# Attention weights times values in a two-layer encoder: padded 128-column values against two 64-column tiles side by side

## What is computed

```python
scores = einsum("bnqkgd,bnskd->bnkgqs", q, kb) * scale        # blocks of 128 queries, up to 3 blocks of keys
scores = where(valid, scores + bias, -inf)                    # window of 128, a slope per head
m = maximum(max(scores, -1), sink_b)
p = exp(scores - m)
denom = sum(p, -1) + exp(sink_b - m)
o = einsum("bnkgqs,bnskd->bnqkgd", p / denom, vb)
```

## Time and profile before

| | us |
|---|---|
| median of 3 runs | 1838.14 (1838.01 to 1838.23) |
| profiled execution, its time | 1838.19 |
| profiled execution, span | 1836.4 |
| granted TensorE clock, mean over the span | 0.997 of 2.4 GHz |
| attention loop, layer 0 | 458.8 to 508.5 of the span |
| attention loop, layer 1 | 1361.8 to 1411.5 of the span |

### The profile page before, as it was taken

One profiled execution on the slowest core, in us unless ns is written; L12 is line 12 of the kernel. 1 busy time (PEld: TensorE's weight loads), 2 busy tenths in 40 slices (PEclk: granted clock), 3 DMA queues, 4 the chain that ended last, 5 costly groups with the idle time before them and its releaser, 6 DMA issues.

```text
span 1836.4 us, 24082 instructions
## 1 busy us (share of the span) xinstructions
PE 1800.0 (98%) x8080; PEld 1477.4 (80%) x8080; DVE 895.9 (49%) x1169; ACT 749.4 (41%) x990; POOL 1062.6 (58%) x533
## 2 busy tenths in 40 slices
PE   7999999999899999999999999999998999999997
PEld 5888888888588888888888888888876888888886
DVE  6545432268776444432254444322797654444223
ACT  6333332246865333332243333223576643333221
POOL 5444457769656444457744444676784854444673
PEclk9999999999999999999999999999999999999998
DMA  4332323321113323223332322333211233222331
GB/s 172 104 102 91 99 71 100 110 98 64 46 47 104 103 91 103 82 79 98 121 104 91 98 96 81 87 101 124 69 47 47 81 103 100 94 92 82 87 100 64
DMA packets 53427, 166.73 MB, mean 91 GB/s; under 512 B 6000, under 2 KB 6256, under 8 KB 53360
## 3 DMA queue, kind: packets, MB, share of 16 engines
q1 hardware_dynamic: 52128, 163.78, 28.3%
q10 hardware_dynamic: 1232, 2.10, 0.3%
HBM read 163.76 MB, written 2.10 MB: 90 GB/s over the span
## 4 chain that ended last, share of the span: by engine, by line
issue 42%; POOL 32%; PE 23%; POOLq 2%; DVE 1%; ACT 1%; DMA 0%; ACTq 0%; DVEq 0%
POOL w_lo L413 26%; PE bank L1211 7%; PE bank L1212 7%; PE bank L1213 7%; POOL y_conv L464 3%; POOL sq_sum L422 2%; POOLq L412 1%; PE bank L1373 1%; POOL x L533 1%; POOL r_wide L489 0%; DVE glu L1146 0%; POOLq L426 0%; DVE result L1201 0%; PE bank L1383 0%; PE bank L1247 0%
## 5 line engine op out<-in xcount | busy, mean ns | idle before, releaser
L413 POOL TENSOR_TENSOR w_lo<-stage,w_hi 128x1024 fp32r<-128x1024 f32 x352 | 871.3, 2476 | 701.8 <-ACT w_hi L548 701.7
L548 ACT ACTIVATE w_hi<-stage 128x1024 fp32r<-128x1024 f32 x352 | 372.4, 1060 | 894.0 <-PE bank L1213 892.5
L1211 PE MATMUL bank<-xs_hi,w_hi 128*128 128x512 f32 (+1 forms) x1704 | 663.5, 389 | 0.0
L1213 PE MATMUL bank<-xs_hi,w_lo 128*128 128x512 f32 (+1 forms) x1704 | 659.7, 387 | 0.0
L1212 PE MATMUL bank<-xs_lo,w_hi 128*128 128x512 f32 (+1 forms) x1704 | 659.6, 387 | 0.0
L1211 PEld LDWEIGHTS bank<-xs_hi,w_hi 128*128 128x128 f32 x1704 | 320.0, 188 | 66.7 <-issue 1.9
L1212 PEld LDWEIGHTS bank<-xs_lo,w_hi 128*128 128x128 f32 x1704 | 320.0, 188 | 66.1 <-issue 1.9
L1213 PEld LDWEIGHTS bank<-xs_hi,w_lo 128*128 128x128 f32 x1704 | 319.9, 188 | 65.8
L845 DVE TENSOR_TENSOR work<-bank,rstd 128x512 f32<-128x512 f32 x176 | 120.9, 690 | 403.6 <-PE bank L1213 402.7
L1211 PE MATMUL bank<-h_hi,w_hi 128*128 128x512 f32 x704 | 273.9, 389 | 0.0
L1212 PE MATMUL bank<-h_lo,w_hi 128*128 128x512 f32 x704 | 273.9, 389 | 0.0
(11 more groups left out here) (151 smaller groups left out, 1221.7 us busy)
## 6 DMA issues: line engine op xcount, KB each, us to landing
stage<-w_gu SPq DMA_DIRECT2D x176, 512.0 KB, 3.3
stage<-w_down SPq DMA_DIRECT2D x64, 384.0 KB, 3.2
stage<-w_down SPq DMA_DIRECT2D x64, 320.0 KB, 2.9
stage<-w_in SPq DMA_DIRECT2D x24, 512.0 KB, 3.3
stage<-w_out SPq DMA_DIRECT2D x16, 512.0 KB, 3.3
x<-xT ACTq DMA_DIRECT2D x4, 512.0 KB, 7.0
stage<-w_in SPq DMA_DIRECT2D x8, 256.0 KB, 2.7
out<-result SPq DMA_DIRECT2D x8, 256.0 KB, 2.2
```

The lines of the kernel that those rows point to most:

```text
L413: nc.gpsimd.tensor_tensor(w_lo[:, r, :], stage[:, r, :], w_hi[:, r, :].bitcast(F32), ALU.subtract).then_inc(split, 1)
L548: nc.scalar.activation(w_hi[:, r, :], stage[:, r, :], ACT.Copy).then_inc(hi_made, 1)
L1211: nc.tensor.matmul(to, wh, mh, start=first, stop=False)
L1213: return nc.tensor.matmul(to, wl, mh, start=False, stop=last)
```

## The change

The values lose their padding. `v` has 128 columns per key block, 64 of each key/value head, copied in one ACT instruction. `weigh_values` now takes a block `b` and does both heads: for each key block a product with 64 columns of weights for kv 0 into partitions 0 to 63 of `side_bank`, and one for kv 1 into partitions 64 to 127, each at its column position of the array. It is called at `c == 2` of groups 2, 4 and 6 (units 10, 18, 26) and once behind the loop, in place of seven calls at `c == 3` and one behind the loop. `pt` has 3 slots instead of 2, and the waits for a free slot count blocks. `o_made` rises once a block. `widen` and `r_wide` go: `spread_denominators` reads each reciprocal as a 64-column broadcast, again in two halves, 8 products instead of 4, and waits for DVE's reciprocals instead of POOL.

```diff
+PT_SLOTS = 3
-WIDEN_IN = [1, 3, 5, 6]
...
-            pt = sb("pt", [P, 2, 3, GROUP, P], F32, region)
+            pt = sb("pt", [P, PT_SLOTS, 3, GROUP, P], F32, region)
...
-            v = sb("v", [P, NB, N_KV_HEADS, P], F32, region)
+            v = sb("v", [P, NB, P], F32, region)
...
-            r_wide = sb("r_wide", [P, GROUP, N_KV_HEADS, HEAD_DIM], F32, region)
...
-                def widen(b):
-
-                    pool.wait_ge(r_den_made, l * NB + b + 1)
-                    if b:
-                        pool.wait_ge(factors_spread, l * NB + b)
-                    for kv in range(N_KV_HEADS):
-                        nc.gpsimd.tensor_tensor(r_wide[:, :, kv, :],
...
-                    if g in WIDEN_IN:
-                        widen(WIDEN_IN.index(g))
...
-                    if g >= 2 and c == 0:
-                        act.wait_ge(o_made, l * N_GROUPS + g - 1)
+                    if g >= PT_SLOTS and c == 0:
+                        act.wait_ge(o_made, l * NB + (g - PT_SLOTS) // 2 + 1)
...
-                    nc.scalar.activation(pt[:, g % 2, 0:n, c, :], src, ACT.Copy).then_inc(pt_made, 1)
+                    nc.scalar.activation(pt[:, g % PT_SLOTS, 0:n, c, :], src, ACT.Copy).then_inc(pt_made, 1)
...
-                for kv in range(N_KV_HEADS):
-                    at = slice(HEAD_DIM * kv, HEAD_DIM * (kv + 1))
-                    nc.scalar.activation(v[:, :, kv, at], side_bank[:].rearrange("p (b d) -> p b d", d=P)[:, :, at],
-                                         ACT.Copy).then_inc(v_made, 1)
+                nc.scalar.activation(v[:], side_bank[:].rearrange("p (b d) -> p b d", d=P), ACT.Copy).then_inc(v_made, 1)
...
-                    dve.wait_ge(o_made, l * N_GROUPS + 2 * b + 2)
+                    dve.wait_ge(o_made, l * NB + b + 1)
...
-                    nc.vector.memset(v[:, :, kv, other], 0.0).then_inc(v_made, 1)
...
-                def weigh_values(g):
+                def weigh_values(b):
...
-                    pe.wait_ge(pt_made, l * N_UNITS + (g + 1) * GROUP)
-                    if b and not kv:
+                    pe.wait_ge(pt_made, l * N_UNITS + (b + 1) * 2 * GROUP)
+                    if b:
                         pe.wait_ge(o_evicted, l * NB + b)
                     for i in range(n):
-                        last = nc.tensor.matmul(side_bank[:], v[:, first + i, kv, :],
-                                                pt[:, g % 2, i, :, :].rearrange("p c q -> p (c q)"),
-                                                start=not kv and i == 0, stop=bool(kv) and i == n - 1)
+                        for kv in range(N_KV_HEADS):
+                            rows = slice(HEAD_DIM * kv, HEAD_DIM * (kv + 1))
+                            last = nc.tensor.matmul(side_bank[rows, :], v[:, first + i, rows],
+                                                    pt[:, (2 * b + kv) % PT_SLOTS, i, :, :].rearrange("p c q -> p (c q)"),
+                                                    start=i == 0, stop=i == n - 1, tile_position=(0, HEAD_DIM * kv))
                     last.then_inc(o_made, 1)
...
-                    pe.wait_ge(r_widened, (l * NB + b + 1) * N_KV_HEADS)
+                    pe.wait_ge(r_den_made, l * NB + b + 1)
                     bank_taken(ATT["spread", b, 0])
                     for c in range(GROUP):
-                        last = nc.tensor.matmul(att_bank("spread", b, 0)[:, c * P:(c + 1) * P],
-                                                r_wide[:, c, :, :].rearrange("p h d -> p (h d)"),
-                                                ident[:], start=True, stop=True)
+                        for kv in range(N_KV_HEADS):
+                            rows = slice(HEAD_DIM * kv, HEAD_DIM * (kv + 1))
+                            last = nc.tensor.matmul(att_bank("spread", b, 0)[rows, c * P:(c + 1) * P],
+                                                    r_den[:, 2 * b + kv, c:c + 1].to_broadcast([P, HEAD_DIM]),
+                                                    ident[:], start=True, stop=True, tile_position=(0, HEAD_DIM * kv))
                     last.then_inc(factors_spread, 1)
...
-                        pe.wait_ge(v_made, l * 4 + 4)
-                    if c == 3 and g:
-                        weigh_values(g - 1)
+                        pe.wait_ge(v_made, l + 1)
+                    if c == 2 and g and g % 2 == 0:
+                        weigh_values(g // 2 - 1)
...
-                weigh_values(N_GROUPS - 1)
+                weigh_values(NB - 1)
```

More of the change, by code:

```diff
@@ L283, in encoder @@
         factors_spread = sem("factors_spread")
-        r_widened = sem("r_widened")
         factors_kept = sem("factors_kept")
@@ L481, in denominators @@
                                             ALU.add).then_inc(den_made, 1)
-                def widen(b):
-                    pool.wait_ge(r_den_made, l * NB + b + 1)
-                    if b:
-                        pool.wait_ge(factors_spread, l * NB + b)
-                    for kv in range(N_KV_HEADS):
-                        nc.gpsimd.tensor_tensor(r_wide[:, :, kv, :],
-                                                r_den[:, 2 * b + kv, :].unsqueeze(2).to_broadcast([P, GROUP, HEAD_DIM]),
-                                                zero[:, 0:1].unsqueeze(2).to_broadcast([P, GROUP, HEAD_DIM]),
-                                                ALU.add).then_inc(r_widened, 1)
                 def add_channel(c):
@@ L1363, in turn_weights @@
                     last.then_inc(turned, 1)
-                def weigh_values(g):
-                    b, kv = divmod(g, 2)
+                def weigh_values(b):
                     first, n = keys_of(b)
-                    pe.wait_ge(pt_made, l * N_UNITS + (g + 1) * GROUP)
-                    if b and not kv:
+                    pe.wait_ge(pt_made, l * N_UNITS + (b + 1) * 2 * GROUP)
+                    if b:
                         pe.wait_ge(o_evicted, l * NB + b)
                     for i in range(n):
-                        last = nc.tensor.matmul(side_bank[:], v[:, first + i, kv, :],
-                                                pt[:, g % 2, i, :, :].rearrange("p c q -> p (c q)"),
-                                                start=not kv and i == 0, stop=bool(kv) and i == n - 1)
+                        for kv in range(N_KV_HEADS):
[3 more added lines that the diff above has]
+                                                    start=i == 0, stop=i == n - 1, tile_position=(0, HEAD_DIM * kv))
```

## The result

The changed kernel takes 1841.67 us (median of 13 runs, 1839.00 to 1842.82) against 1838.14 before (13 runs, 1837.70 to 1838.55). The ratio is 1.0018, with a 95% interval of 1.0010 to 1.0025. Its runs spread over 3.8 us, those of before over 0.85. The three fastest, 1839.0 to 1839.5, have a mean granted clock of 0.993; the other ten, 1840.3 to 1842.8, have 0.991 or 0.992. The profiled execution took 1842.45 us, span 1840.6, clock 0.991; before, 1838.19 and 0.997.

What follows compares the result with a forecast made beforehand. PE, busy 98% of the span, was taken to bound the kernel, with ACT pacing the loop's start. A gain of 5.8 or 2.2 us over two layers, middle 4.0, took 1838.19 to 1834.2 us; range 1831 to 1852.

Steps and rivals of the forecast that it cites:

- TensorE's clock falls: Rival, chance 0.12: PE nearly empty between about 489.5 and 496, its clock drops; +2 to +4 us, 1842 to 1846.
- The overlap: Value products: both heads run at once in the array's halves, between full and staggered; with steady clock, chance 0.52.
- full: Value products: both heads wholly side by side, 1.72 us for two key blocks, 2.58 for three; gain 2.9 a layer.
- staggered: Value products: only a head's second record runs beside the other's first; 2.15 and 3.01 us, gain 1.1 a layer.
- The toll of changing shape: Rival, chance 0.08: fill, drain or exposed weight loads eat 1 to 2 us a layer, 1836 to 1839.
- The spread: Spread of the denominators on PE: 16 records with 64 weight columns take 1.0 us, lower bound half; before, 0.99.
- at these stations nothing is: Reciprocals for the spreads: DVE makes them at units 4, 13, 21, 25, PE needs them at 10, 18, 25, 31; none late.
- the walk: Eight stations through a layer's attention loop, by the slowest at each: gain 2.9 or 1.1 us a layer.
- Stations 1 to 4 of the walk: Loop from unit 10's scores to unit 31's scores: these end at 487.2 or 488.1; before, 488.37.
- Station 5: DVE's last taps, 8.3 us to the channel sum, then PE's mean, starting at 495.9 or 496.8; before, 499.11.
- Stations 6 to 8: Product of block 2, ACT's last copies, last product: ends at 505.5 or 507.3; before, 508.42.
- The sum: Whole kernel: 1838.19 less 4.0 us, the middle of 5.8 and 2.2 for both layers, gives 1834.2 us.

Runs made afterwards that it cites:

- the swapped loops: The changed kernel with a block's loops exchanged, all key blocks of one head before the other's, still 64-column tiles: 1844.90 us, ratio 1.0035.
- the repaired kernel: The changed kernel with three filling products ahead of the mean and POOL's last `w_lo` of the loop waiting for DVE's channel sum: 1833.24 us, ratio 0.9969.
- the spread alone: The kernel before with only the new `spread_denominators`, without `widen`; value products stay padded in their old places: 1832.50 us, ratio 0.9969.

## Why the prediction was wrong

It named 1834.2 us; the kernel came out slower than before, at 1841.67, next to the rival *TensorE's clock falls* (1842 to 1846), which had a chance of 0.12. That the number lies so near this rival is in part luck: the rival had no collision in it, and with the collision taken away the fallen clock leaves 1836.75 us, faster than before.

**The overlap: right, and better than taken.** The step took the middle of full and staggered. It is full: 1.77 and 2.62 us against 1.72 and 2.58. "Strict order", on which staggered rested, does not hold across halves, as the swapped loops show. The Trainium skill's 2.38 times for three tiles (TensorE: Matmul & The Clock Gate, Part 3) agrees in kind: two fp32 tiles give 5.24 / 2.62 = 2.0. The same part of the Trainium skill calls matmuls strictly first in, first out in start and end. Here the records of the spread that start ahead of the last value product contradict that, and the measurement decides.

**The toll of changing shape: right to be small.** What follows each pair of blocks starts within 0.1 us. The drain at a change of tiling mode, which that skill states (TensorEngine Tiling, Key Properties), is not seen as more than this.

**The spread: right.** 16 records take 0.97 us; 1.0 was taken. The lower bound of 0.5 was not reached. But "at these stations nothing is", said of reciprocals that come late, was wrong for the third spread: PE waits 2.40 us for `r_den` there (to 491.88). DVE's list has that reciprocal behind the run of taps that unit 31's scores start. This is the first of the two idle stretches around the fall of the clock, and the walk has no station for it.

**Stations 1 to 4 of the walk: right with full overlap.** These stations agree with the walk within 0.13 us. Unit 10's scores end at 471.0 (471.1 said); unit 11's turn starts at 473.77 (473.9); the product of block 1 starts at 482.90 (482.8); unit 31's scores end at 487.24 (487.2). The gain there is 1.1 us (488.37 less 487.24), as the walk had it.

**Station 5 failed: the mean.** "These scores start DVE's last run of taps, 8.3 us from 488.66 to the channel sum" carried a duration over from a row in which DVE's sum met only the end of a `w_lo` of POOL. With the old product gone from the stretch behind unit 31's scores, ACT and after it POOL reach the last `w_lo` just ahead of the sum, which takes 2.72 us and not 1.10. The mean starts at 497.56, not 495.9. What the engines freed by a product that moves will do next, and with whom they collide, was not asked. Taking the collision away is worth 4.9 us, and with the clock held 2.8 by the medians or 4.5 to 4.8 between like groups of runs.

**Stations 6 to 8 failed: the durations.** The mean and the product of block 2 were priced at the clock of the trace before. The rival had the mechanism, the place ("between about 489.5 and 496") and about the price: 4 us for the two. Measured, from the mean's start to the end of the product, they take 6.86 us (497.56 to 504.42) against 3.90 with the clock held (497.39 to 498.67 and 2.62), so 3.0 more in layer 0 of the profiled executions. Holding the clock is worth 5.6 us in all. What was wrong is its chance. It was held down by "the clock has stood at 1.00 through the whole loop with 15 to 20% of idle time", a share over long windows (it is 12 to 23% in the first three of the earlier trace rows and none in the last), when the walk itself left PE only turns and one spread in more than six microseconds. Before, PE was busy for 8.26 of the 10.70 us of that window; now 3.72. The Trainium skill has the clock fall back when the array goes idle (TensorE: Matmul & The Clock Gate, Part 1); the trace agrees, in both layers: the granted clock is 0.73 and 0.77 in the last two stretches of layer 0 and 0.80 and 0.69 in those of layer 1.

**The sum.** With both failures taken away the arrangement of the change measures 1833.24 us, 1.0 below the forecast, and at full overlap the walk had 1838.19 - 5.8 = 1832.4. So the size of the gain was about right once both failures are away, though the repaired kernel has a sum of 0.69 us where the walk had 1.10; 8.4 us of loss, two terms that the sum lacked, turned its sign.

**Which part brings what** was not forecast apart, and should have been: the spread alone brings 5.6 us, as much as the whole walk. The value products, 8.6 us of PE work less in a layer, bring little or nothing on top (1833.24 repaired, with three of seven runs near 1831.2, against 1832.50). One reason that the runs show is their place: ahead of unit 31's scores they delay DVE, which waited 2.58 us there. With block 1's product moved behind them, block 2's ahead of the mean and the collision off the last `w_lo`, the kernel is 4.0 us below the spread alone.

## What to carry to other kernels

An engine that is made faster leaves idle stretches, and two things happen in them that the trace before cannot show as rows: TensorE's clock may fall, and neighbours meet that used to pass one another. So after a walk by due times, list the idle stretch of PE that it predicts, and give its successors the price at both clock levels. And place the shortened work by who waits behind it. Ahead of a late input it costs nothing, though alone it did not keep the clock up here. Ahead of the scores that another engine waits for, or behind the mean, it delays the whole tail.

## What the runs showed of the hardware

- fp32 products with 64-column weights in the two halves of the array run fully side by side: 12 records of 512 columns in 2.62 us against 5.24 for the same on 128 columns. Records of one half start ahead of earlier ones for the other (the swapped loops, 1.76 us for two key blocks and 3.55 for three).
- PE idled 2.40 us, ran a spread of 1.1 us and idled 4.58 us. The granted clock fell at the start of the second idle stretch (1.00 up to 493.00, mean 0.52 from there to 497.56); the twelve records behind took 4.43 us in place of 2.62. A filling product of 0.86 us and five more ahead of the mean kept it at 1.00 and made the kernel 5.6 us faster. With the product of block 2 right behind the spread the long second stretch was gone from there, and the clock fell all the same in layer 0 (0.50 from 493.00 to 496.00) but not at that place in layer 1 of the same execution, so the same idle stretch of 2.40 us ahead does not decide it.
- DVE's sum of two SBUF tensors (128x512) took 0.69 us with POOL idle, 1.10 and 1.88 in two kernels where it started 1.80 and 1.04 us after the start of a `w_lo`, and 2.72 when it started 0.17 us after the start of one of 2.34. In the changed kernel the `w_lo` ends at 496.96 and the sum at 497.51, 0.55 us later; in the other two the sum ends 0.54 us after the `w_lo`. So DVE waits for POOL's instruction to end. The Trainium skill (SBUF — State Buffer, Who interferes with whom) has the port pair that VectorE and GpSimd share as the only place of contention, an exclusive lock, and says that an instruction of VectorE with two SBUF inputs contends with one of GpSimd that reads SBUF. The trace agrees.
